# A 31-tap depthwise convolution: one of two channel tiles from TensorE to VectorE

## The reference, cut to what matters

```
z = h @ w_in                       # 256 x 1024 times 1024 x 3088, split by columns
a, g = split(c_glu, 2)             # 256 channels each
hc = causal_dwconv(a * sigmoid(g), conf_conv_w, conf_conv_b)   # 31 taps, one filter a channel
hc = silu(layernorm(hc) * ln_w + ln_b)
...                                # mLSTM branch and forgetting attention (log_f = log_sigmoid(...))
x  = x + concat([hm, hc, hf]) @ w_out
```

## Time and profile before

| | |
|---|---|
| time, median of 3 runs (lowest, highest) | 2595.77 us (2594.27 to 2596.47) |
| the profiled execution: its own time | 2595.33 us |
| its span (first to last instruction) | 2593.4 us |
| mean granted TensorE clock | 0.979 of full speed |
| busy: PE, DVE, ACT | 2468.5, 1834.1, 1540.3 us |

### The profile page before, as it was taken

The page is one execution under the profiler, slowest core; times in us unless marked ns, Lnnn a source line. Parts: engine busy times, 40 slices in busy tenths (PEclk is TensorE's granted clock), DMA queues, the critical chain, the costliest instruction groups (busy, mean ns, idle before and its releaser), DMA issues.

```text
span 2593.4 us, 39051 instructions
## 1 busy us (share of the span) xinstructions
PE 2468.5 (95%) x15246; PEld 2101.5 (81%) x15246; DVE 1834.1 (71%) x2516; ACT 1540.3 (59%) x2000; POOL 27.9 (1%) x85
## 2 busy tenths in 40 slices
PE   8998899999999899999899999897999999999997
PEld 5866688888886788898788889687888888888886
DVE  5547767566565766664576656466998998998997
ACT  4255466455445566545565545565777777777775
POOL 0000000000000000010000001000000000000000
PEclk9998999999999899999999999899999999999999
DMA  8244345555543545554135545133999999999995
GB/s 324 98 147 170 135 151 195 181 184 187 193 148 131 211 164 186 187 181 147 66 131 183 190 179 197 50 131 143 360 359 354 358 359 354 358 360 351 359 361 205
DMA packets 81579, 565.73 MB, mean 218 GB/s; under 512 B 9280, under 2 KB 12608, under 8 KB 13568
## 3 DMA queue, kind: packets, MB, share of 16 engines
q1 hardware_dynamic: 80112, 559.95, 58.2%
q0 software_dynamic: 1296, 3.38, 0.5%
HBM read 559.92 MB, written 1.05 MB: 216 GB/s over the span
## 4 chain that ended last, share of the span: by engine, by line
PE 82%; DVE 9%; ACT 6%; issue 2%; DMA 1%; SPq 0%; ACTq 0%; DVEq 0%
PE psum L236 80%; DVE ring_lo L230 3%; ACT ring_hi L227 2%; DVE hT L788 1%; PE psum L711 1%; PE psum L2096 1%; DVE hT L1358 1%; DMA Z<-in_first_mods 1%; ACT hT L752 1%; ACT Z L760 1%; DVE hT L432 0%; DVE Z L1332 0%; DVE Z L1331 0%; DVE mixT L629 0%; DVE Z L1323 0%
## 5 line engine op out<-in xcount | busy, mean ns | idle before, releaser
L230 DVE TENSOR_TENSOR ring_lo<-ring,ring_hi 128x2048 fp32r<-128x2048 f32 x479 | 1096.8, 2291 | 307.1 <-ACT ring_hi L227 301.8
L227 ACT ACTIVATE ring_hi<-ring 128x2048 fp32r<-128x2048 f32 x479 | 916.3, 1914 | 339.7 <-PE psum L236 334.8
L236 PE MATMUL psum<-h_parts,ring_hi 128*128 128x512 f32 (+1 forms) x3184 | 863.8, 351 | 18.7 <-DVE h_parts L442 5.4
L236 PE MATMUL psum<-h_parts,ring_lo 128*128 128x256 f32 (+1 forms) x2464 | 603.4, 291 | 0.0
L236 PEld LDWEIGHTS psum<-h_parts,ring_hi 128*128 128x128 f32 x3184 | 518.2, 191 | 43.6 <-issue 17.0
L236 PE MATMUL psum<-ring_hi,h_parts 128*128 128x512 f32 (+1 forms) x1952 | 540.2, 363 | 5.5 <-DVE h_parts L440 3.7
L236 PEld LDWEIGHTS psum<-h_parts,ring_lo 128*128 128x128 f32 x2464 | 468.3, 190 | 72.5
L236 PEld LDWEIGHTS psum<-ring_hi,h_parts 128*128 128x128 f32 x1952 | 345.1, 190 | 56.7 <-issue 4.1
L236 PE MATMUL psum<-ring_lo,h_parts 128*128 128x512 f32 (+1 forms) x976 | 352.5, 361 | 0.0
L236 PE MATMUL psum<-ring_hi,Zr 128*128 128x512 f32 x704 | 219.3, 393 | 0.0
L236 PEld LDWEIGHTS psum<-ring_lo,h_parts 128*128 128x128 f32 x976 | 184.9, 189 | 28.2
(11 more groups left out here) (282 smaller groups left out, 2282.8 us busy)
## 6 DMA issues: line engine op xcount, KB each, us to landing
ring<-in_stream SPq DMA_DIRECT2D x524, 1024.0 KB, 4.8
Z<-in_first_mods SPq DMA_DIRECT2D x5, 1024.0 KB, 16.7
mixT<-mixT POOLq DMA_DIRECT2D x32, 71.0 KB, 5.6
cst<-in_constants SPq DMA_DIRECT2D x1, 1216.0 KB, 7.3
xT<-in_xT SPq DMA_DIRECT2D x1, 1024.0 KB, 5.8
xT<-in_ctxT SPq DMA_DIRECT2D x1, 1024.0 KB, 8.1
xT<-in_memT POOLq DMA_DIRECT2D x1, 1024.0 KB, 6.2
out_y<-hT SPq DMA_DIRECT2D x2, 512.0 KB, 3.0
```

Source lines behind the costliest of these rows:

```text
L227: e.activation(hi, raw, ACT.Copy).then_inc(sem("piece_rounded"), 1)
L230: e.tensor_tensor(lo, raw, hi.bitcast(F32), ALU.subtract).then_inc(sem("piece_split"), 1)
L236: ins = pe.matmul(*args, **kw)
```

## The change

For channel tile 1, the convolution leaves PE. DVE computes it as 31 multiply-adds on 128 x 256, one per tap, on two accumulators in turn (`z2(7)` for even taps, `other_taps` for odd ones), and adds the two at the end, which signals `conv_out`. Each tap from the third waits until all but the one just before it have ended. The taps are spread over `between(g)`: 5 each after groups 4 and 5, 2 each after groups 6 to 9, 4 after groups 10 and 12, 5 and the final add after group 13. In each of these steps they come ahead of what DVE did there. Channel tile 0 stays on PE with 32 of its weight blocks. POOL still issues 16 DMAs, each with half the bytes. The weight piece still has the weights of both tiles. The filter weights of tile 1 go into the table of per-partition vectors (31 more columns a layer).

```
-B2_COLS = dict(norm_mix=8, m_conv_w=16, m_conv_b=4, gate_b=16, m_norm=2, c_conv_b=2,
+B2_COLS = dict(norm_mix=8, m_conv_w=16, m_conv_b=4, gate_b=16, m_norm=2, c_conv_b=2, c_taps=31,
                ln_w=2, ln_b=2, norm_x=8, norm_mem=8, norm_ffn=8)
...
# pe_mixer, at group CONV
-                    for c in range(2):
-                        for m in range(8):
-                            for q in range(4):
-                                at = ((c * 4 + q) * 8 + m) * 32
-                                mm(pe, bank[5][32 * q:32 * q + 32, c * T:(c + 1) * T], w[:, at:at + 32],
-                                   CPS[:, c, q, 4 * m:4 * m + T], start=m == 0, stop=m == 7,
-                                   last_of="conv_sums" if m == 7 and q == 3 else None)
+                    for m in range(8):
+                        for q in range(4):
+                            at = (q * 8 + m) * 32
+                            mm(pe, bank[5][32 * q:32 * q + 32, 0:T], w[:, at:at + 32],
+                               CPS[:, 0, q, 4 * m:4 * m + T], start=m == 0, stop=m == 7,
+                               last_of="conv_sums" if m == 7 and q == 3 else None)
...
# act_mixer, at group CONV
-                    for c in range(2):
-                        await_next(act, "conv_sums")
-                        act.activation(z2(6 + c), bank[5][:, c * T:(c + 1) * T], ACT.Identity,
-                                       bias=v("c_conv_b", layer, c, c + 1)).then_inc(sem("conv_out"), 1)
+                    await_next(act, "conv_sums")
+                    act.activation(z2(6), bank[5][:, 0:T], ACT.Identity,
+                                   bias=v("c_conv_b", layer, 0, 1)).then_inc(sem("conv_out"), 1)
...
+        other_taps = mixflat[:, 3200:3200 + T]
+        TAPS_AT = {4: (0, 5), 5: (5, 10), 6: (10, 12), 7: (12, 14), 8: (14, 16), 9: (16, 18), 10: (18, 22), 12: (22, 26),
+                   13: (26, TAPS)}
+
+        def dve_taps(dve, layer, first, end):
+
+            done = layer * TAPS
+            if first == 0:
+                dve.wait_ge(sem("product_out_dve"), gated_outs[layer])
+            for j in range(first, end):
+                y = (z2(7), other_taps)[j % 2]
+                x, w = CP[:, 1, j:j + T], v("c_taps", layer, j, j + 1)
+                if j >= 2:
+                    dve.wait_ge(sem("tap_added"), done + j - 1)
+                if j == 0:
+                    ins = dve.tensor_scalar(y, x, w, v("c_conv_b", layer, 1, 2), ALU.mult, ALU.add)
+                elif j == 1:
+                    ins = dve.tensor_scalar(y, x, w, None, ALU.mult)
+                else:
+                    ins = dve.scalar_tensor_tensor(y, x, w, y, ALU.mult, ALU.add)
+                ins.then_inc(sem("tap_added"), 1)
+            if end == TAPS:
+                dve.wait_ge(sem("tap_added"), done + TAPS)
+                dve.tensor_tensor(z2(7), z2(7), other_taps, ALU.add).then_inc(sem("conv_out"), 1)
...
# dve_mixer, after the step of group 3 and ahead of those of groups 6 to 13
+                if g in TAPS_AT:
+                    dve_taps(dve, layer, *TAPS_AT[g])
...
# POOL
-                        pool.dma_start(CPS[32 * shift:32 * shift + 32, :, q, :],
-                                       CP[32 * q:32 * q + 32, :, shift:shift + 284]).then_inc(sem("shifted"), 16)
+                        pool.dma_start(CPS[32 * shift:32 * shift + 32, 0, q, :],
+                                       CP[32 * q:32 * q + 32, 0, shift:shift + 284]).then_inc(sem("shifted"), 16)
```

More of the change, by code:

```diff
@@ L2790 @@
         put("m_conv_w", l, columns(i["mlstm_conv_w_2"][l]))
+        put("c_taps", l, columns(np.ascontiguousarray(np.asarray(i["conf_conv_w_2"][l]).reshape(TAPS, 2 * P)[:, P:])))
         put("m_conv_b", l, columns(i["mlstm_conv_b_2"][l]))
```

## The result

| | before | after |
|---|---|---|
| median of 5 runs (lowest, highest) | 2595.77 us (2592.56 to 2598.84) | 2608.26 us (2601.30 to 2609.90) |
| ratio, 95% interval | | 1.0044 (1.0031 to 1.0056) |
| the profiled execution: time, span | 2595.33, 2593.4 us | 2609.48, 2606.3 us |
| mean granted TensorE clock | 0.979 | 0.974 |

The change makes the kernel slower by 12.5 us by the medians, 0.5%. The forecast was 2603.7 us, slower by 7.9, with a range up to 2609.5.

A forecast was written before the change was run, and what follows sets the result against it. PE's own matmuls were taken to bound the kernel. Late `log_f` (1.55 us) plus the clock's drop (2.4 us), for two layers, made 7.9 us: 2603.2 us for the profiled execution, 2603.7 as median, range 2597.5 to 2609.5.

The forecast's parts named there:

- The saving: PE's convolution in each mixer: 64 of 128 matmuls go, which takes 3.5 us a layer from PE's work.
- The tap's step: DVE's taps: each starts 0.396 us after the one before, as in L2283; 0.523 us kept for the range.
- The rival with the linked step: DVE's taps step by 0.523 us instead of 0.396, all on the path to `log_f`: 2611 us, chance 0.09.
- Log-sigmoid late by 7.3 us: First layer on DVE: 22 taps ahead of the log-sigmoid move L838 from 1166.60 to 1173.9.
- ACT's part: First layer: exp follows DVE's signal directly at 1174.1, rounding of the next piece comes at 1175.8, DVE's split after it.
- `log_f`: Log-sigmoid's result, L1762 at 1184.05: PE waits 5.1 us at the sums and goes on 1.55 us later than before.
- The clock: PE behind its wait for `log_f`: 4.8 us of matmuls at half speed cost 2.4 us a layer.
- It counts the same: Second layer's mixer: same program at the same distances, so the same loss as in the first layer.
- The wider vector table: Table 62 columns wider, 32 KB copied once: counted as nothing, 0.2 us at most.
- shifted as a whole: Behind PE's sums: no slack gives the delay back; the chain through group 23 and ACT to the barrier moves unchanged.
- my own case: Main forecast, `log_f` late and the clock falling in PE's wait: 2600 to 2608 us, chance 0.60.
- The rival that the taps hide: Taps fit DVE's idle time in the mixers and PE's saving stays: 2588.7 us, chance 0.07.

## Why the prediction was right, and where it fell short

The direction and the mechanism up to the end of the mixers came out as forecast, nearly number for number. The total of the forecast, +7.9 us, is too small against +12.5 and +13.9 measured, for a reason that stands last but one in this list.

- **The saving**: 3.5 us a layer forecast; 60.14 - 56.68 = 3.46 in the run without tile 1.
- **The tap's step**: 0.396 us taken from L2283, 0.396 measured, as the mean of the 44 steps between neighbouring taps in both layers (1150.61 - 1150.21 is one). The rival with the linked step is out. The prediction held this against a rule of the Trainium skill (VectorE: DVE Perf Modes, "The DRAIN you can't avoid"), that the next DVE operation doesn't start until the pipe is empty. That was half a reading: the same section goes on that a next operation that is not held starts earlier. The trace agrees with that second sentence: a tap starts 0.08 us before the listed end of the one in front (step 0.396 us, duration 0.48).
- **Log-sigmoid late by 7.3 us**: L838 at 1173.9 forecast, 1172.70 + 1.04 = 1173.74 measured, 7.1 late. (The 1.04 us are this execution's lead at the start of the stage.)
- **ACT's part**: rounding at 1175.8 forecast, 1174.58 + 1.04 = 1175.6 measured. The table load ahead of the wait is there to see.
- **`log_f`**: L1762 at 1184.05 forecast, 1182.81 + 1.04 = 1183.85. PE's wait: 5.1 us forecast, 4.7 measured. PE later at the sums: 1.55 forecast, 1183.13 + 1.04 - 1182.74 = 1.43 measured.
- **The clock**: 2.4 us a layer forecast, from the wait of 4.9 us in the trace of before, behind which PE worked 4.8 us at half clock; 2.5 and 3.1 by the run that kept PE busy. PE worked 5.6 and 6.9 us at half clock here, so a wait of nearly the same length (4.72 and 4.73) was followed by half clock of different lengths. "It counts the same" did not hold for the second layer.
- **The wider vector table**: nothing was counted, and nothing is seen; the first part of the program took 1147.43 and 1147.63 us in the changed kernel, 1148.47 before.
- **The mixers in sum**: 7.9 us forecast, 8.5 measured.
- **What fell short** is the step "shifted as a whole". I took it that behind the mixer everything keeps its length. In both profiles the four later stages took 6.1 to 6.2 us more, at a lower clock. (In three of them the clock falls in the kernel before too; in the first cross-attention it doesn't.) That is larger than the gap between 2603.7 and 2608.3; the first and the last part of the program gave 1.8 us back in that execution. A step for this loss is missing from the sum, and my own case, 2600 to 2608, just misses the median. The full range, to 2609.5, held it by luck: its upper end stood there for a linked tap or a clock loss of 4.8 us in one layer, and neither came. The second measurement, +13.9 us, lies beyond even that end (+13.7).
- **The rival that the taps hide** was wrong for this order of the taps and right for another one: DVE had the idle time, but only behind what ACT and PE wait for.

What stays open: what decides where the clock falls in the attentions and the router, and so what part of the 6 us is the change's doing. It repeated in the two profiles of the changed kernel, but these are executions of nearly the same time (2609.48 and 2609.22 us) among ten that took from 2601.3 to 2613.9. It is no plain function of the shift in the medians either, since three kernels with about 1.5 us of shift in the first mixer (1.54, 1.56, 1.46) ended 10.2, 2.7 and 0.0 us above the kernel before. (In the second mixer, two of them shifted by 1.5 us as well and one by 3.0.)

## What to carry to other kernels

Before work is moved to an engine with idle time, follow who waits for the instructions that it is put ahead of: here 22 multiply-adds stood in front of three tiny instructions whose result ACT needed, ACT stood in front of DVE's next split, and nine more in front of the result that PE needed. The same 31 instructions in the same idle time, put behind those, turned +12.5 us into -7.5. And count a wait of the matmul engine twice: for its length, and for the clock behind it (here 4.7 us of waiting cost another 2.5 to 3.1).

## What was not expected of the hardware

- The first attention, with the same instructions and the same busy time of DVE (32.2 to 32.6 us), took from 62.7 to 68.1 us over the twelve profiles, with a mean PE clock from 0.97 to 0.85; the second took 62.9 to 69.3. The part of the program ahead of the first mixer, the same in all of them, took from 1147.1 to 1153.1.
- Work that nobody reads can pay: 39 matmuls in a wait of 4.7 us saved 2.5 and 3.1 us in the mixers, and the kernel as a whole ran some 13 us faster.
- Waits of 1.29 and 1.54 us behind the convolution of 32-column matmuls were followed by a lower clock in the second layer (mean 0.97 over the mixer), while waits of 1.30 and 1.53 us at the same place of the first layer were not.
